# A two-layer decoder step on one core: filler products during the first loads, the first weight unit in three parts, the second unit ahead of the memory rows

## The chip, the cores and the metric

The kernel runs on one core of a Trainium2 chip. The metric is device time in microseconds (us), as the median of several runs; a measurement of this kernel can tell a difference of about 0.2% from none. A profile covers one further execution.

## What is computed

One inference step of a decoder trunk with two layers, for 256 prompt tokens and 64 sample tokens (320 columns in all) that share the weights. The part that matters here is the first layer's mixer:

```
z = x @ w_in[l] -> [q | k | v | conv h | conv B | conv C | mem q | gate_a | gate_c | gate_m]
A: sliding-window grouped-query attention with sinks
B: short gated convolution
M: 4-head cross-attention into N_MEM=256 memory tokens
   mk = mem_prompt @ w_mem_k[l];  mv = mem_prompt @ w_mem_v[l]      (256x1024 @ 1024x256, both layers)
m = sig(gate_a)*(A @ p_attn) + sig(gate_c)*(B @ p_conv) + sig(gate_m)*(M @ p_mem)
x <- LayerNorm(ALPHA * x + m @ w_o)
x <- LayerNorm(ALPHA * x + ffn(x))     dense in layer 0, 2 of 8 experts in layer 1
```

All is float32. Each product is made of three TensorE products of split operands (a high and a low part of the weights and of the activations): high x high, low weights x high, high weights x low.

## The kernel before, in words

**Units.** The weights are streamed as units of 1 MB (128 partitions x 2048 words), in the order of the list `STREAM`: two z units (each 256 columns of w_in), the four memory units (mk and mv of both layers), the other z units with p_conv, p_mem, p_attn and w_o, then the dense feed-forward, layer 1's mixer and the experts. Unit n goes into slot n mod 6 (`RING`) of `raw`. SyncE (`sp`, L653) issues the loads in that order; from the sixth on it waits until the unit that had the slot is used up (`unit_done`).

**The split of a unit.** For each unit ScalarE writes the rounded high part (`hi`, L932) and then VectorE the remainder (`lo`, L1320) in place of the raw words. Both run two units ahead of TensorE (`AHEAD`), and ScalarE's first waits until the unit three before is used up. So at the head of step i of `mixer` stand `hi(n + 2)` on ScalarE and `lo(n + 2)` on VectorE, ahead of the rest of the step.

**The start.** x arrives by three loads (two of 128 prompt rows, one of 64 sample rows). TensorE turns it in six parts of four 128-column transposes (`start_part`, L1923; k = 0, 1, 2 are the first halves of the three row blocks, 3 to 5 the second halves), ScalarE copies the high part of each (L947) and VectorE the low part (L1330). The first weight unit comes in two halves (`HALVES`), each split by ScalarE (L953) and VectorE (L1337). The memory rows (`mstage`) are loaded ahead of the second unit and turned by TensorE between the first and the second unit, in four parts more.

**The steps.** In `mixer(0)` TensorE multiplies the z units one after the other (48 products of 320 columns each). After the first it turns the memory rows; after the second (i = 1) comes `memory()`, the products of the four memory units (48 each, of 256 columns). Attention runs beside the z units: the table `SLOTS` says what follows which step. For the first of nine attention jobs (prompt rows 0 to 127 against the memory keys) it has: scores at step 1, an unrelated set of transposes of cached keys (`memk`) at step 2, and at step 3 the transposes of its probabilities (`probs`, L2004), which need the exponentials of ScalarE (L1012) and the normalisation of VectorE (L1414, L1415). VectorE does that normalisation at the next step, behind that step's `lo`.

**Banks.** Results of z units go to banks 0, 1, 2 in turn. A product into a bank waits until ScalarE has copied out the tile that was there three before (`z_cp`).

```
for i, u in enumerate(layer_units(l)):      # ScalarE
    hi(n + AHEAD)
    z_copy(l, 2 * u[2]); z_copy(l, 2 * u[2] + 1)
    ...
    if l == 0 and i == 1:
        memory()
    for work in SLOTS.get(i, ()):
```

Of the kernel before, what the change touches and what calls it, by code (L numbers as in the profile page):

```python
# [55 lines left out]
RING = 6  # L56
HI_RING = 3

HALVES = (slice(0, UNIT // 2), slice(UNIT // 2, UNIT))
RING_MOE = 11  # L60
AHEAD = HI_RING - 1

# [23 lines left out]


MEM_UNITS = [(k, l, 0) for k in ("mk", "mv") for l in range(2)]
STREAM = layer_units(0)[:2] + MEM_UNITS + layer_units(0)[2:] + ffn_units() + layer_units(1)
N_DENSE = len(STREAM)  # L90
UNIT_OF = {u: n for n, u in enumerate(STREAM)}

# [109 lines left out]
LAST_VALUES = ("pv", NJ - 1)  # L202
BETWEEN_TILES = next(i for i in SLOTS if LAST_VALUES in SLOTS[i])
assert SLOTS[BETWEEN_TILES] == [LAST_VALUES] and layer_units(0)[BETWEEN_TILES][0] == "z"
EVENTS = [x[1:] for w in sorted(SLOTS) for x in SLOTS[w] if x[0] == "event"]
N_EVENTS = len(EVENTS)
EVENT_NO = {e: n for n, e in enumerate(EVENTS)}
# [38 lines left out]
def build_trunk(nc, A, O):  # L246
    with ExitStack() as ctx:
# [20 lines left out]
        def sem(name):  # L268
            return ctx.enter_context(nc.semaphore(name))
# [178 lines left out]
        unit_done = sem("unit_done")  # L448
        zeroed = sem("zeroed")
        ld_x = [sem(f"ld_x{t}") for t in range(3)]  # L450
        ld_first = [sem(f"ld_first{h}") for h in range(2)]
        first_hi = sem("first_hi")
        first_lo = sem("first_lo")
        ld_mem = sem("ld_mem")
# [198 lines left out]

        @block.sync
        def _(sp):
            for t in range(2):
                sp.dma_start(xstage[:, t, :], A["x_prompt"][0, 128 * t:128 * t + 128, :]).then_inc(ld_x[t], 16)
            sp.dma_start(xstage[0:64, 2, :], A["x_sample"].rearrange("b t d -> (b t) d")).then_inc(ld_x[2], 16)
            for h in range(2):
                ks = slice(4 * h, 4 * h + 4)  # L660
                sp.dma_start(tiled(raw[0], 256)[:, ks], unit_source(STREAM[0])[:, ks]).then_inc(ld_first[h], 16)
            for n, u in enumerate(STREAM):
                if n == 0:
                    continue
                if n == 1:
                    for t in range(2):
                        sp.dma_start(mstage[:, t, :], A["mem_prompt"][0, 128 * t:128 * t + 128, :]).then_inc(ld_mem, 16)
                s = n % RING
# [85 lines left out]
        def _(pool):  # L754
# [34 lines left out]
                               A["cache_mem_v"][l, 4 * g:4 * g + 4].rearrange("b (k p) h d -> p (b k) (h d)", p=P)  # L789
                               ).then_inc(ld_memv, 16)  # L790

            pool.wait_ge(ld[UNIT_OF[MEM_UNITS[-1]]], 16)
            load_mem_k(0, 0)
            load_mem_v(0, 0)
            for l in range(2):
# [127 lines left out]
        def _(act):  # L923
# [22 lines left out]
                src = ps[:, bank, :].rearrange("p (f t) -> p f t", t=P)[:, :, 0:tn]  # L946
                act.activation((xh if k < X_STARTS else mTh)[:, f:f + 4, t0:t0 + tn], src, ACT.Copy).then_inc(start_hi, 1)  # L947

            for h, done in ((0, first_hi), (1, hi_done)):
                for k in range(3 * h, 3 * h + 3):  # L950
                    start_part(k)
                act.wait_ge(ld_first[h], 16)
                act.activation(high[0][:, HALVES[h]], raw[0][:, HALVES[h]], ACT.Copy).then_inc(done, 1)  # L953
            hi(1)
            act.wait_ge(const, CONSTS)

# [160 lines left out]
            def mixer(l):  # L1117
                units = layer_units(l)
                for i, u in enumerate(units):
                    n = UNIT_OF[u]  # L1120
                    hi(n + AHEAD)
                    if u[0] == "z":
                        z_copy(l, 2 * u[2])
                        if i == BETWEEN_TILES:
                            o_copy(l, NJ - 1)
                        z_copy(l, 2 * u[2] + 1)
                        if i == BETWEEN_TILES:
                            continue
                        if u[2] == 9:
                            act.wait_ge(conv_done, l + 1)  # L1130
                            act.activation(och[:, :, :], hbc[:, 4:6, :], ACT.Copy).then_inc(och_done, 1)
                    if l == 0 and i == 0:
                        for k in range(X_STARTS, len(START)):
                            start_part(k)
                        continue
                    if l == 0 and i == 1:
                        memory()
                    for work in SLOTS.get(i, ()):
                        if work[0] == "pv" and JOBS[work[1]][0] == "smem":
                            by_token(l, work[1])  # L1140
                        elif work[0] in ("pv", "turn"):
                            o_copy(l, work[1])
                        elif work[0] == "event":
                            event_copy(l, work[1:])
                        else:
                            exps(l, work[1])
                    if u[0] == "pattn":
                        for f in range(4 * u[2], 4 * u[2] + 4):
                            act.wait_ge(merge_done, l * len(MERGES) + MERGE_NO[("pattn", f)] + 1)
                            act.activation(xh[:, f, :], merged[:, f, :], ACT.Copy, scale=0.5).then_inc(mh_done, 1)  # L1150
                    if u[0] == "wo" and u[2] >= 1:
                        if u[2] == 1:
# [144 lines left out]
        def _(dve):  # L1297
# [32 lines left out]
                dve.tensor_tensor(low_part[:, f:f + 4, t0:t0 + tn], src,  # L1330
                                  high_part[:, f:f + 4, t0:t0 + tn].bitcast(F32), ALU.subtract).then_inc(start_lo, 1)

            for h, (before_it, done) in enumerate(((first_hi, first_lo), (hi_done, lo_done))):
                for k in range(3 * h, 3 * h + 3):
                    start_part(k)
                dve.wait_ge(before_it, 1)
                dve.tensor_tensor(low[0][:, HALVES[h]], raw[0][:, HALVES[h]],  # L1337
                                  high[0][:, HALVES[h]].bitcast(F32), ALU.subtract).then_inc(done, 1)
            lo(1)

            def masks():
# [218 lines left out]
            def mixer(l):  # L1560
                pending = None
                for i, u in enumerate(layer_units(l)):
# [11 lines left out]
                    if u[0] in ("pconv", "pmem"):  # L1574
                        for f in range(KD):
                            merge(l, u[0], f)
                    if l == 0 and i == 0:
                        for k in range(X_STARTS, len(START)):
                            start_part(k)
                    lo(UNIT_OF[u] + AHEAD)  # L1580
                    if l == 0 and i == 0:
                        continue
                    if l == 0 and i == 1:
                        memory()
                    if u == ("z", l, 8):
                        conv(l)
# [2 lines left out]
                    if pending is not None:  # L1589
                        normalise(l, pending)  # L1590
                        pending = None
                    for work in SLOTS.get(i, ()):
                        if work[0] == "turn" or work[0] == "pv" and JOBS[work[1]][0] != "smem":
                            o_low(l, work[1])
                        elif work[0] == "scores":
                            scores(l, work[1])
                            pending = work[1]
# [307 lines left out]
        def _(pe):  # L1905
# [20 lines left out]

            pe.wait_ge(const, 1)
            for k in range(X_STARTS):
                pe.wait_ge(ld_x[k % 3], 16)
                start_part(k)  # L1930

# [240 lines left out]
            def mixer(l):  # L2172
                for i, u in enumerate(layer_units(l)):
# [25 lines left out]
                    if side_by_side:  # L2199

                        qs = [OUT_NO[tile] for tile in tiles]
                        for k in range(KD):
                            if n == 0 and k % 4 == 0:
                                pe.wait_ge(start_lo, 3 * (k // 4) + 3)
                            if n == 0 and k == KD // 2:
                                pe.wait_ge(lo_done, 1)
                            if i > 0:
                                pe.wait_ge(ml_done, KD * l + k + 1)
# [22 lines left out]
                            first_mean(2 * l)  # L2231
                    if l == 0 or i > 1:
                        last.then_inc(unit_done, 1)
                    if l == 0 and i == 0:
                        pe.wait_ge(ld_mem, 2 * 16)
                        for k in range(X_STARTS, len(START)):
                            start_part(k)
                        continue
                    if l == 0 and i == 1:
                        memory()  # L2240
                    for work in SLOTS.get(i, ()) if i != BETWEEN_TILES else ():
                        if work[0] == "pv":
                            values(l, work[1])
                        elif work[0] == "turn":
                            turn_values(l, work[1])
                        elif work[0] == "event":
                            event(l, work[1:])
                        else:
                            scores(l, work[1])
# [272 lines left out]
```

## Time and profile before

| what | value |
|---|---|
| median of 3 runs | 1553.41 us (1552.87 to 1554.34) |
| the profiled execution | 1552.14 us |
| its span, first to last instruction | 1550.4 us |
| TensorE busy | 1520.2 us, 98% |
| VectorE, ScalarE, GpSimd busy | 1123.1, 927.2, 146.7 us |
| moved by DMA | 416.62 MB, mean 269 GB/s |

The profiled execution lies 1.27 us under the median of the runs, and 1.7 us of it lie around its span. Times in the trace are from the start of the span. "PE" is TensorE's products, "PEld" its weight loads, DVE VectorE, ACT ScalarE, SP SyncE. The listed length of a product contains its way through the array, so products that follow one another overlap: what one costs is the distance between two starts.

### The profile page before, as it was taken

Reading aid. Unit: us, or ns where it says so; the run is one execution under the profiler, and the core shown is the slowest. Engines: PE = TensorE matmul, PEld = TensorE weight load, DVE = VectorE, ACT = ScalarE, POOL = GpSimd, SP = SyncE. Lnnn points to the kernel's source line nnn. Section 1 sums busy time; section 2 is a strip of 40 time slices with the busy share of each in tenths; the row PEclk is TensorE's granted clock in tenths of the full one; section 3 lists DMA queues with packets and bytes.
Section 4 is the critical chain, followed back from the end, with each engine's and each line's share of the span. In section 5 each row is a group of like instructions: output and inputs, shape, how many; then the busy total and the mean of one; then the engine's idle time right before and its main releaser. Section 6 shows DMA issues by size and latency. Waiting matters only on the chain.

```text
span 1550.4 us, 22897 instructions
## 1 busy us (share of the span) xinstructions
PE 1520.2 (98%) x9065; PEld 1345.9 (87%) x9065; DVE 1123.1 (72%) x1044; ACT 927.2 (60%) x974; POOL 146.7 (9%) x182
## 2 busy tenths in 40 slices
PE   8999999999999999999899999999999999999996
PEld 7999999999999899999588888888888888888785
DVE  5546658844443536558698888888888888889987
ACT  5445445533333644544677777777777777777775
POOL 3203003300002103002230000000000000020000
PEclk9999999999999999999999999999999999999998
DMA  9845534695444346332799999999999999999981
GB/s 317 275 134 183 163 121 145 243 360 161 131 150 157 110 150 183 110 111 81 272 391 389 395 390 357 386 382 389 369 353 380 388 386 369 356 384 380 389 297 61
DMA packets 226425, 416.62 MB, mean 269 GB/s; under 512 B 8592, under 2 KB 110368, under 8 KB 224752
## 3 DMA queue, kind: packets, MB, share of 16 engines
q1 hardware_dynamic: 217712, 383.28, 70.2%
q0 software_dynamic: 8608, 31.89, 5.7%
q8 instruction: 73, 1.20, 0.3%
q14 instruction: 32, 0.26, 0.0%
HBM read 393.99 MB, written 23.11 MB: 269 GB/s over the span
## 4 chain that ended last, share of the span: by engine, by line
PE 95%; DVE 2%; ACT 1%; DMA 0%; issue 0%; POOL 0%; SPq 0%; DVEq 0%; POOLq 0%; ACTq 0%
PE ps L1908 13%; PE ps L1910 13%; PE ps L1909 13%; PE ps L2441 11%; PE ps L2443 11%; PE ps L2442 10%; PE ps L2425 5%; PE ps L2427 5%; PE ps L2426 5%; PE ps L2452 1%; PE ps L2004 1%; PE ps L1975 1%; PE ps L1943 0%; PE ps L1945 0%; PE ps L1944 0%; PE ps L2032 0%
## 5 line engine op out<-in xcount | busy, mean ns | idle before, releaser
L1310 DVE TENSOR_TENSOR low<-raw,high 128x2048 fp32r<-128x2048 f32 x264 | 603.8, 2291 | 88.2 <-ACT high L939 86.8
L939 ACT ACTIVATE high<-raw 128x2048 fp32r<-128x2048 f32 x264 | 505.9, 1919 | 199.8 <-PE ps L2443 126.8
L1320 DVE TENSOR_TENSOR low<-raw,high 128x2048 fp32r<-128x2048 f32 (+1 forms) x91 | 206.7, 2274 | 195.7 <-ACT high L932 195.6
L1908 PE MATMUL ps<-xh,high 128*128 128x320 f32 x1056 | 331.8, 314 | 4.3 <-DVE xl L1533 2.7
L1909 PE MATMUL ps<-xh,low 128*128 128x320 f32 x1056 | 327.0, 310 | 0.0
L1910 PE MATMUL ps<-xl,high 128*128 128x320 f32 x1056 | 326.9, 310 | 0.0
L2441 PE MATMUL ps<-high,xeh 128*128 128x512 f32 (+1 forms) x768 | 291.8, 380 | 2.7 <-ACT row_f L1239 2.5
L2443 PE MATMUL ps<-high,xel 128*128 128x512 f32 (+1 forms) x768 | 288.7, 376 | 0.0
L2442 PE MATMUL ps<-low,xeh 128*128 128x512 f32 (+1 forms) x768 | 287.5, 374 | 0.0
L932 ACT ACTIVATE high<-raw 128x2048 fp32r<-128x2048 f32 (+1 forms) x91 | 172.2, 1892 | 144.1 <-PE ps L1910 120.4
L1908 PEld LDWEIGHTS ps<-xh,high 128*128 128x128 f32 x1056 | 199.3, 189 | 10.9 <-issue 9.5
L1909 PEld LDWEIGHTS ps<-xh,low 128*128 128x128 f32 x1056 | 199.5, 189 | 0.2
L1910 PEld LDWEIGHTS ps<-xl,high 128*128 128x128 f32 x1056 | 199.1, 189 | 0.0
L2441 PEld LDWEIGHTS ps<-high,xeh 128*128 128x128 f32 x768 | 144.4, 188 | 31.3 <-issue 2.7
L2443 PEld LDWEIGHTS ps<-high,xel 128*128 128x128 f32 x768 | 144.2, 188 | 28.9
L2442 PEld LDWEIGHTS ps<-low,xeh 128*128 128x128 f32 x768 | 144.1, 188 | 27.4
L2425 PE MATMUL ps<-high,heh 128*128 128x512 f32 x352 | 141.2, 401 | 0.0
L2427 PE MATMUL ps<-high,hel 128*128 128x512 f32 x352 | 138.4, 393 | 0.0
L2426 PE MATMUL ps<-low,heh 128*128 128x512 f32 x352 | 138.4, 393 | 0.0
L2427 PEld LDWEIGHTS ps<-high,hel 128*128 128x128 f32 x352 | 66.3, 188 | 15.3
L2425 PEld LDWEIGHTS ps<-high,heh 128*128 128x128 f32 x352 | 66.2, 188 | 14.2 <-issue 0.2
L2426 PEld LDWEIGHTS ps<-low,heh 128*128 128x128 f32 x352 | 66.3, 188 | 13.7
(388 smaller groups left out, 1664.8 us busy)
## 6 DMA issues: line engine op xcount, KB each, us to landing
raw<-in_exp_w_gate_dram SPq DMA_DIRECT2D x88, 1024.0 KB, 7.7
raw<-in_exp_w_up_dram SPq DMA_DIRECT2D x88, 1024.0 KB, 7.7
raw<-in_exp_w_down_dram SPq DMA_DIRECT2D x88, 1024.0 KB, 7.1
raw<-in_w_in_dram SPq DMA_DIRECT2D x37, 1024.0 KB, 5.3
ybuf<-zeros POOLq DMA_DIRECT2D x12, 1024.0 KB, 19.7
raw<-in_ffn_w_gate_dram SPq DMA_DIRECT2D x11, 1024.0 KB, 5.4
raw<-in_ffn_w_up_dram SPq DMA_DIRECT2D x11, 1024.0 KB, 6.5
raw<-in_w_o_dram SPq DMA_DIRECT2D x8, 1024.0 KB, 5.1
```

The costliest lines, as they stand in the source:

```text
L939: act.activation(high[(N_DENSE + m) % HI_RING][:, :], raw_moe[s][:, :], ACT.Copy).then_inc(hi_done, 1)
L1310: dve.tensor_tensor(low_moe[s][:, :], raw_moe[s][:, :], high[(N_DENSE + m) % HI_RING][:, :].bitcast(F32), ALU.subtract).then_inc(lo_done, 1)
L1320: dve.tensor_tensor(low[n % RING][:, cols], raw[n % RING][:, cols], high[n % HI_RING][:, cols].bitcast(F32), ALU.subtract).then_inc(lo_don ...
L1908: pe.matmul(out, wh, ah, start=first, stop=False)
L1909: pe.matmul(out, wl, ah, start=False, stop=False)
L1910: return pe.matmul(out, wh, al, start=False, stop=last)
L2425: pe.matmul(out, heh[:, tile, :], wh[:, c], start=i == 0 and k == 0, stop=False)
L2426: pe.matmul(out, heh[:, tile, :], wl[:, c], start=False, stop=False)
L2427: last = pe.matmul(out, hel[:, tile, :], wh[:, c], start=False, stop=i == NBLK - 1 and k == 1)
L2441: pe.matmul(out, xeh[:, k, slots], wh[:, c], start=k == 0, stop=False)
L2442: pe.matmul(out, xeh[:, k, slots], wl[:, c], start=False, stop=False)
L2443: last = pe.matmul(out, xel[:, k, slots], wh[:, c], start=False, stop=k == KD - 1)
```

## The change

- TensorE multiplies the identity by itself (128x128) ahead of the first three start parts, 6, 2 and 4 times, with a result that nothing reads (`WARM_UP`).
- The first unit is loaded and split in three parts (k = 0 and 1, 2 and 3, 4 to 7). The first of them is loaded ahead of the sample rows, and ScalarE and VectorE split a part between the start parts. TensorE begins the unit when the first part is split.
- SyncE loads the second unit ahead of the memory rows, and the third z unit ahead of the four memory units.
- TensorE turns the memory rows behind the second unit instead of the first, and `memory()` follows the third unit (i = 2). What `SLOTS` had for step 1 and step 2 of layer 0 now both follows step 2.

```
-HALVES = (slice(0, UNIT // 2), slice(UNIT // 2, UNIT))
+FIRST_PARTS = ((0, 2), (2, 4), (4, KD))
+FIRST_COLUMNS = tuple(slice(256 * k0, 256 * k1) for k0, k1 in FIRST_PARTS)
+WARM_UP = (6, 2, 4)
...
-STREAM = layer_units(0)[:2] + MEM_UNITS + layer_units(0)[2:] + ffn_units() + layer_units(1)
+STREAM = layer_units(0)[:3] + MEM_UNITS + layer_units(0)[3:] + ffn_units() + layer_units(1)
...
+def beside(l, i):
+
+    if l == 0 and i < 3:
+        return SLOTS[1] + SLOTS[2] if i == 2 else []
+    return SLOTS.get(i, [])
...
             for t in range(2):
                 sp.dma_start(xstage[:, t, :], A["x_prompt"][0, 128 * t:128 * t + 128, :]).then_inc(ld_x[t], 16)
+            first_part(0)
             sp.dma_start(xstage[0:64, 2, :], A["x_sample"].rearrange("b t d -> (b t) d")).then_inc(ld_x[2], 16)
-            for h in range(2):
-                ks = slice(4 * h, 4 * h + 4)
-                sp.dma_start(tiled(raw[0], 256)[:, ks], unit_source(STREAM[0])[:, ks]).then_inc(ld_first[h], 16)
+            first_part(1)
+            first_part(2)
...
-                if n == 1:
+                if n == 2:
                     for t in range(2):
                         sp.dma_start(mstage[:, t, :], A["mem_prompt"][0, 128 * t:128 * t + 128, :]).then_inc(ld_mem, 16)
...
+            start_part(0)
+            start_part(1)
+            first_part(0, first_hi)
+            start_part(2)
+            first_part(1, first_hi)
+            for k in range(3, 6):
+                start_part(k)
+            first_part(2, hi_done)
...
-                    if l == 0 and i == 0:
+                    if l == 0 and i == 1:
                         for k in range(X_STARTS, len(START)):
                             start_part(k)
-                        continue
-                    if l == 0 and i == 1:
+                    if l == 0 and i == 2:
                         memory()
-                    for work in SLOTS.get(i, ()):
+                    for work in beside(l, i):
...
             for k in range(X_STARTS):
+                for _ in range(WARM_UP[k] if k < 3 else 0):
+                    pe.matmul(ps[:, 1, 0:P], ident[:, :], ident[:, :], start=True, stop=True)
                 pe.wait_ge(ld_x[k % 3], 16)
                 start_part(k)
```

Three places in the order of the instructions. The first is the start of the program on TensorE, before and after; `xstage` holds the rows of x, `ident` the identity.

```order
L1904 UNCONDITIONAL_BRANCH
L1923 MATMUL ps<-ident,xstage 128x128 x8
L1923 MATMUL ps<-ident,xstage 128x64 x4
L1923 MATMUL ps<-ident,xstage 128x128 x8
L1923 MATMUL ps<-ident,xstage 128x64 x4
```

```order
L1932 UNCONDITIONAL_BRANCH
L1958 MATMUL ps<-ident 128x128 x6
L1951 MATMUL ps<-ident,xstage 128x128 x4
L1958 MATMUL ps<-ident 128x128 x2
L1951 MATMUL ps<-ident,xstage 128x128 x4
L1958 MATMUL ps<-ident 128x128 x4
L1951 MATMUL ps<-ident,xstage 128x64 x4
L1951 MATMUL ps<-ident,xstage 128x128 x8
L1951 MATMUL ps<-ident,xstage 128x64 x4
```

Twelve identity products have come in between; all 24 transposes still stand ahead of the first product of the first unit.

The second place is TensorE behind the last product of the memory units: before, then now. L2025 (now L2055) are the scores of the first attention job, L1975 (L2005) the transposes of cached keys, L2004 (L2034) those of the job's probabilities; each left-out stretch is one z unit.

```order
L2025 MATMUL ps<-mkT,qmT 128x256 x4
L1908 MATMUL ps<-xh,high_61 128x320
...
L1975 MATMUL ps<-ident,kstage 128x128 x8
L1908 MATMUL ps<-xh,high_62 128x320
...
L2004 MATMUL ps<-ident,sc 128x128 x8
```

```order
L2055 MATMUL ps<-mkT,qmT 128x256 x4
L2005 MATMUL ps<-ident,kstage 128x128 x8
L1936 MATMUL ps<-xh,high_62 128x320
...
L2034 MATMUL ps<-ident,sc 128x128 x8
```

Between the scores and the transposes of the probabilities stand one z unit now, and two before.

The third place is ScalarE at the same point, from the copy of the second layer's memory keys on: before, then now. `sc<-ps` are the exponentials of the first job, `mem_kT` the copy of the turned cached keys, `high` the high part of a unit.

```order
L963 ACTIVATE mkT<-ps 128x512
L932 ACTIVATE high_62<-raw_50 128x2048
L1012 ACTIVATE sc,small<-ps,small 128x256 x4
L932 ACTIVATE high_63<-raw_51 128x2048
L1038 ACTIVATE qT<-ps 64x256
...
L970 ACTIVATE mem_kT<-ps 128x1024
```

```order
L985 ACTIVATE mkT<-ps 128x512
L947 ACTIVATE high_63<-raw_51 128x2048
L1034 ACTIVATE sc,small<-ps,small 128x256 x4
L992 ACTIVATE mem_kT<-ps 128x1024
L947 ACTIVATE high_61<-raw_52 128x2048
L1063 ACTIVATE kvT<-ps 128x320 x2
```

The copy of the cached keys now stands between the exponentials and the next high part. On VectorE the rows are the same as before there: low part of that unit, then reciprocal and normalisation.

## Rows read from the trace of the kernel before

**Rows 1.** The page: busy times; the chain that ended last, by engine.
```profile
PE 1520.2 (98%) x9065; PEld 1345.9 (87%) x9065; DVE 1123.1 (72%) x1044; ACT 927.2 (60%) x974; POOL 146.7 (9%) x182
...
PE 95%; DVE 2%; ACT 1%; DMA 0%; issue 0%; POOL 0%; SPq 0%; DVEq 0%; POOLq 0%; ACTq 0%
```

**Rows 2.** Waits of PE, whole span: total, times, longest, in us.
```profile
PE ps L1908 <- DVE xl L1533: 2.7, 1, 2.7
```

**Rows 3.** Timeline of PE, 0 to 23 us: start, length, instructions [idle before them].
```profile
4.57 1.09 PE L1923 MATMUL ps<-ident,xstage 128*128 128x128 f32 x4 [4.57 <-DMA xstage<-in_x_prompt_dram]
...
8.55 3.20 PE L1923 MATMUL ps<-ident,xstage 64*128 64x64 f32 x16 [1.36 <-DMA xstage<-in_x_sample_dram]
12.22 0.61 PE L1908 MATMUL ps<-xh,high 128*128 128x320 f32 x1 [0.48 <-issue]
...
15.56 0.45 PE L1908 MATMUL ps<-xh,high 128*128 128x320 f32 x1
15.83 0.34 PE L1909 MATMUL ps<-xh,low 128*128 128x320 f32 x1
...
20.99 1.91 PE L1923 MATMUL ps<-ident,mstage 128*128 128x128 f32 x16
22.65 0.39 PE L1908 MATMUL ps<-xh,high 128*128 128x320 f32 x1
```

**Rows 4.** Windows: busy us of PE, PEld, DVE, ACT, POOL; PEclk, DMA share, GB/s.
```profile
6.00:8.00 2.00, 1.12 (x4) 0.72 (x4) 0.84 (x2) 0.89 (x2) 0.72 (x2) 1.00 0.97 218
8.00:10.00 2.00, 1.45 (x8) 1.33 (x9) 0.86 (x2) 0.57 (x2) 0.00 (x0) 1.00 1.11 354
```

**Rows 5.** Timelines of ACT and DVE, 9 to 23 us.
```profile
9.81 1.06 ACT L953 ACTIVATE high<-raw 128x1024 fp32r<-128x1024 f32 x1 [0.15 <-DMA raw<-in_w_in_dram]
...
20.17 1.92 ACT L932 ACTIVATE high<-raw 128x2048 fp32r<-128x2048 f32 x1 [1.15 <-DMA raw<-in_w_mem_k_dram]
...
22.25 0.43 ACT L1050 ACTIVATE qm_diag<-ps 64x64 f32<-64x64 f32 x2
...
9.69 0.42 DVE L1330 TENSOR_TENSOR xl<-ps,xh 128x256 fp32r<-128x256 f32 x1 [1.14 <-ACT xh L947]
10.90 1.23 DVE L1337 TENSOR_TENSOR low<-raw,high 128x1024 fp32r<-128x1024 f32 x1 [0.79 <-ACT high L953]
```

**Rows 6.** Timeline of PE, 53 to 70 us: from the first scores to their probabilities.
```profile
53.65 1.14 PE L2025 MATMUL ps<-mkT,qmT 64*128 64x256 f32 x8
54.71 0.41 PE L1908 MATMUL ps<-xh,high 128*128 128x320 f32 x1
...
61.86 1.04 PE L1975 MATMUL ps<-ident,kstage 128*128 128x128 f32 x8
62.65 0.39 PE L1908 MATMUL ps<-xh,high 128*128 128x320 f32 x1
...
69.77 0.49 PE L2004 MATMUL ps<-ident,sc 128*128 128x128 f32 x3
```

**Rows 7.** Timeline of DVE, 54 to 67 us.
```profile
54.36 0.23 DVE L1367 COPY vecs<-ps 128x76 f32<-128x76 f32 x1
...
57.35 1.22 DVE L1381 TENSOR_REDUCE small<-ps 128x4 f32<-128x1024 f32 x1
...
62.58 2.29 DVE L1320 TENSOR_TENSOR low<-raw,high 128x2048 fp32r<-128x2048 f32 x1 [3.80 <-ACT high L932]
...
64.99 1.22 DVE L1415 TENSOR_TENSOR sc<-sc,small 128x1024 f32<-128x1024 f32 x1
```

**Rows 8.** Timeline of ACT, 60 to 66 us.
```profile
60.63 1.92 ACT L932 ACTIVATE high<-raw 128x2048 fp32r<-128x2048 f32 x1
...
64.59 1.03 ACT L970 ACTIVATE mem_kT<-ps 128x1024 f32<-128x1024 f32 x1
```

**Rows 9.** The end: PE's last product (timeline); one window with its PEclk.
```profile
1536.02 0.39 PE L2395 MATMUL ps<-ygl,slot 128*128 128x512 f32 x1
...
1541.00:1542.00 1.00, 0.00 (x0) 0.00 (x0) 1.00 (x1) 1.00 (x3) 0.00 (x0) 0.81 0.00 0
```

More of the change, by code:

```diff
@@ L450, in build_trunk @@
         ld_x = [sem(f"ld_x{t}") for t in range(3)]
-        ld_first = [sem(f"ld_first{h}") for h in range(2)]
+        ld_first = [sem(f"ld_first{h}") for h in range(3)]
         first_hi = sem("first_hi")
@@ L655, in _, with first_part @@
         def _(sp):
+            def first_part(h):
+                ks = slice(*FIRST_PARTS[h])
+                sp.dma_start(tiled(raw[0], 256)[:, ks], unit_source(STREAM[0])[:, ks]).then_inc(ld_first[h], 16)
             for t in range(2):
                 sp.dma_start(xstage[:, t, :], A["x_prompt"][0, 128 * t:128 * t + 128, :]).then_inc(ld_x[t], 16)
+            first_part(0)
             sp.dma_start(xstage[0:64, 2, :], A["x_sample"].rearrange("b t d -> (b t) d")).then_inc(ld_x[2], 16)
-            for h in range(2):
-                ks = slice(4 * h, 4 * h + 4)
-                sp.dma_start(tiled(raw[0], 256)[:, ks], unit_source(STREAM[0])[:, ks]).then_inc(ld_first[h], 16)
+            first_part(1)
+            first_part(2)
             for n, u in enumerate(STREAM):
@@ L790, in load_mem_v @@
                                ).then_inc(ld_memv, 16)
-            pool.wait_ge(ld[UNIT_OF[MEM_UNITS[-1]]], 16)
+            pool.wait_ge(ld[UNIT_OF[MEM_UNITS[-1]] % RING], LD_VALUE[UNIT_OF[MEM_UNITS[-1]]])
             load_mem_k(0, 0)
@@ L947, in start_part, with first_part @@
                 act.activation((xh if k < X_STARTS else mTh)[:, f:f + 4, t0:t0 + tn], src, ACT.Copy).then_inc(start_hi, 1)
-            for h, done in ((0, first_hi), (1, hi_done)):
-                for k in range(3 * h, 3 * h + 3):
-                    start_part(k)
+            def first_part(h, done):
                 act.wait_ge(ld_first[h], 16)
-                act.activation(high[0][:, HALVES[h]], raw[0][:, HALVES[h]], ACT.Copy).then_inc(done, 1)
+                act.activation(high[0][:, FIRST_COLUMNS[h]], raw[0][:, FIRST_COLUMNS[h]], ACT.Copy).then_inc(done, 1)
+            start_part(0)
[6 more added lines that the diff above has]
+            first_part(2, hi_done)
             hi(1)
@@ L1331, in start_part, with first_part @@
                                   high_part[:, f:f + 4, t0:t0 + tn].bitcast(F32), ALU.subtract).then_inc(start_lo, 1)
[L1333 to L1338, printed above, removed]
+            def first_part(h, done):
+                c = FIRST_COLUMNS[h]
+                dve.tensor_tensor(low[0][:, c], raw[0][:, c], high[0][:, c].bitcast(F32), ALU.subtract).then_inc(done, 1)
+            start_part(0)
+            start_part(1)
+            dve.wait_ge(first_hi, 1)
+            first_part(0, first_lo)
+            start_part(2)
+            dve.wait_ge(first_hi, 2)
+            first_part(1, first_lo)
+            for k in range(3, 6):
+                start_part(k)
+            dve.wait_ge(hi_done, 1)
+            first_part(2, lo_done)
             lo(1)
@@ L1576, in mixer @@
                             merge(l, u[0], f)
-                    if l == 0 and i == 0:
+                    if l == 0 and i == 1:
                         for k in range(X_STARTS, len(START)):
@@ L1580, in mixer @@
                     lo(UNIT_OF[u] + AHEAD)
-                    if l == 0 and i == 0:
-                        continue
-                    if l == 0 and i == 1:
+                    if l == 0 and i == 2:
                         memory()
@@ L1591, in mixer @@
                         pending = None
-                    for work in SLOTS.get(i, ()):
+                    for work in beside(l, i):
                         if work[0] == "turn" or work[0] == "pv" and JOBS[work[1]][0] != "smem":
@@ L2204, in mixer @@
                                 pe.wait_ge(start_lo, 3 * (k // 4) + 3)
-                            if n == 0 and k == KD // 2:
+                            if n == 0 and k == FIRST_PARTS[1][0]:
+                                pe.wait_ge(first_lo, 2)
+                            if n == 0 and k == FIRST_PARTS[2][0]:
                                 pe.wait_ge(lo_done, 1)
@@ L2233, in mixer @@
                         last.then_inc(unit_done, 1)
-                    if l == 0 and i == 0:
+                    if l == 0 and i == 1:
                         pe.wait_ge(ld_mem, 2 * 16)
@@ L2237, in mixer @@
                             start_part(k)
-                        continue
-                    if l == 0 and i == 1:
+                    if l == 0 and i == 2:
                         memory()
-                    for work in SLOTS.get(i, ()) if i != BETWEEN_TILES else ():
+                    for work in beside(l, i) if i != BETWEEN_TILES else ():
                         if work[0] == "pv":
```

## The prediction

> **What bounds the kernel now.** I read the page first. TensorE is busy for 98% of the span, and 95% of the chain that ended last is its work [rows 1]. So time can go only where TensorE idles or runs slowly, and whatever makes it wait anew is added to the end one for one. The list of TensorE's waits came next. Its longest wait outside the start is 2.7 us, at a layer norm [rows 2]; that one is measured from TensorE's own last product, so it moves with TensorE and absorbs nothing. No transfer comes at a fixed time later on either: SyncE's loads wait for units that TensorE has used up.
>
> The timeline of TensorE shows what the start costs. Nothing runs until 4.57 us, when the first rows of x are there. The sample rows land at 8.55 us; from then 16 transposes take 3.20 us, and the first product of the first unit starts at 12.22 us [rows 3]. At that moment the low part of the unit's first half has just ended on VectorE (10.90 + 1.23 = 12.13) [rows 5]. The first products start 0.27 us apart: 13 lie between 12.22 and 15.83 us (0.267 us each for 320 columns, which is the level of 1.2 GHz), and the remaining 35 take 5.16 us, 0.147 us each, the level of 2.4 GHz [rows 3]. The column of the granted clock reads 1.00 at 6 to 10 us already [rows 4], so here the spacing is the evidence and not that column. Transposes did not raise the rate: 24 of them ran between 4.57 and 11.75 us.
>
> The last place is where the change joins two steps of attention. Scores of the first job start at 53.65, TensorE reaches the transposes of its probabilities at 69.77 [rows 6], and VectorE has had them ready since 64.99 + 1.22 = 66.21 us [rows 7]. That slack of 3.6 us is what I set against the unit that the change takes out from between.
>
> **The start, part by part.** The 12 identity products cost no more than the idle time in which they stand. A 128-column transpose takes about (1.09 - 0.42) / 3 = 0.22 us at the low rate [rows 3]; the identity products have the same shape, so I take 0.22 us and double it as an upper bound. Six are 1.3 us (bound 2.6) inside the 4.57 us before x. Two are 0.45 us and four 0.9 us (bounds 0.9 and 1.8) ahead of the next two landings; the gap before the sample rows is 1.36 us [rows 3] and they now land later, so nothing is pushed by more than 0.4 us even at the bounds.
>
> Loads: 256 KB of the first unit now pass ahead of the sample rows. At 354 GB/s that is 0.74 us, at 218 GB/s 1.2 us [rows 4], and nothing if the transfers in flight share the engines anyway. I take 0.4 us: sample rows at 8.95 us. All 16 transposes behind them still stand ahead of the first unit. At the low rate they end at 8.95 + 3.20 = 12.15 us. The first part of the unit is then long split (it needs half of 1.06 + 1.23 us behind its landing [rows 5]), so the three parts take VectorE's work off this path, but the path through the transposes is as long. First product at 12.15 instead of 12.22: a gain of **0.1 us**, between -0.7 and +0.4.
>
> The rest of the head: the second unit lands before the memory rows instead of behind them, which is earlier than it is needed. The 16 transposes of the memory rows (1.66 us, from 20.99 to 22.65 [rows 3]) move behind the second unit, the third unit (7.1 us) moves ahead of the memory units: neither is added or removed. SyncE issues one load more, hidden, since its queue is ahead of the engines. GpSimd's load of cached keys waits for the last memory unit, which is now the seventh unit; the keys are first needed after all memory units, some 20 us behind that landing. Cost nothing; without that cover it would be what the load is late by.
>
> **The joined steps.** From the start of the scores, TensorE needs 54.71 - 53.65 = 1.06 us for them, 62.65 - 61.86 = 0.79 for the cached keys and 69.77 - 62.65 = 7.12 for one z unit [rows 6]: it reaches the probabilities 8.97 us behind the start of the scores. The cached keys' transposes also need VectorE's copy that ends at 54.36 + 0.23 = 54.59 us [rows 7]; TensorE gets there at 54.71, so this costs about nothing.
>
> The other engines' chain starts at the same moment. VectorE first ends the sum of x and reduces the scores from 57.35 us [rows 7]; exponentials; then ScalarE makes the next unit's high part from 60.63 us for 1.92 us, VectorE its low part (62.58, 2.29 us) and only then the normalisation, ready at 66.21, 12.56 us behind the scores [rows 7, 8]. Nothing in that chain is shortened, and one thing is put in: ScalarE's copy of the cached keys (1.03 us listed, about 0.95 in a row of others [rows 8]) now stands between the exponentials and that high part. So the probabilities are ready 12.56 + 0.95 + 0.1 (signalling) = 13.6 us behind the scores. TensorE waits 13.6 - 8.97 = **4.6 us**; bounds 4.4 and 4.8. Queued behind it are the next scores and unit four, all on the chain. Later jobs keep their two units of distance, so the wait comes once and isn't won back.
>
> **Sum.** Against the profiled execution: 1552.14 + 4.6 - 0.1 = 1556.6 us. The median of the runs lies 1.27 us above that execution, which I carry over: 1553.41 + 4.5 = **1557.9 us**.
>
> **Where a rule speaks otherwise.** The trace shows a rate that stayed low through transposes and rose 3.6 us after the first true product [rows 3]. The Trainium skill, page "TensorE: Matmul & The Clock Gate" (Part 4), says that transposes don't count as activity for the clock gate; by that rule, the trace agrees, and the identity products, which are no transposes, could count. The same page (Part 1) says that the moment of the rise differs from run to run, which the one execution here can't show. By the rule the start could run at the high rate; that is the first rival, worked out from rows.
>
> **Rivals.**
> *A, the rate is high when the sample rows land.* Then 16 transposes take 1.66 us [rows 3], first product near 8.95 + 1.7 = 10.7 us (the sample rows' low part, 1.56 us behind the landing by 10.11 - 8.55, allows it [rows 3, 5]). First unit 48 x 0.147 = 7.1 us, to 17.8. But the second unit's second tile needs a bank that ScalarE frees only behind the third unit's high part: if that unit lands where the third one did, at 20.17, the copy ends at 22.25 + 0.43 = 22.7 us [rows 5]; half a unit behind it is 26.2. Before, two units would end at 20.99 + 7.1 = 28.1. Gain 1.9 us, at most 3.2 if the landing is earlier: 1553.41 + 4.6 - 1.9 = 1556.1, down to 1554.8. For: products were issued. Against: they fill 0.22 x 12 = 2.6 of the first 9 us, in three bursts with idle time between. Chance 0.29.
> *B, the clock falls during the new wait.* At the end of the span TensorE's last product ends at 1536.4, and the window 1541 to 1542 reads 0.81, so the fall from 2.4 to 1.2 GHz came near 1541.6, 5.2 us later [rows 9]; a wait of 2.7 us [rows 2] did nothing of the kind. 4.6 us lie between. If it falls, the next 13 products or twice as many cost 0.12 us more each: 1.6 to 3.1 us, 1559.5 to 1561.0. Chance 0.12.
> *C, faster: the wait is covered.* The place is the transposes of the first job's probabilities. It would need the normalisation to be ready 9.0 us behind the scores rather than 13.6, by VectorE or ScalarE being some 4.6 us less late than their queues show. Then only the start's gain is left, with the high rate 1.9 us or more: 1551.5, down to 1550.2. For it speaks only that the slack before was 3.6 us; against, that a whole unit of 7.1 us leaves the stretch. Chance 0.07.
> *D, the change does little of what it says:* some of the wait is covered and the start is unchanged, 1553.5 to 1556. Chance 0.06.
>
> **The numbers.** Forecast 0.46. Slower by over 0.2% is above 1556.5 us: nearly all of the forecast (0.43), B (0.12) and a third of A (0.10) make 0.65. Within 0.2%: the rest of A (0.19), of the forecast (0.03) and D, 0.28. Faster: C, 0.07. The range goes from 1554.3, which leaves out C and a little of A and D, to 1560.3, which leaves out the upper half of B.
>
> **What would show it.** Right: an idle time of TensorE of 4.4 to 4.8 us at the transposes of the first probabilities (L2034), released by VectorE's normalisation; the first 320-column product near 12.15 us, with a spacing of 0.27 us for about 3.6 us. A would show as a spacing of 0.147 us from the first product on. B would show as 0.27 us spacing in the unit behind the wait. The prediction is wrong if TensorE passes L2034 without idling, if the start gives more than 2 us, or if a new wait stands at the second unit or at the memory units.

## The result, and the profile after

| | before | changed |
|---|---|---|
| median, 7 runs each | 1553.41 us | 1559.14 us |
| lowest and highest | 1552.10 to 1555.54 | 1558.03 to 1559.57 |
| span of the profiled execution | 1550.4 us | 1557.4 us |

The ratio to the kernel before is 1.0037, 95% interval 1.0027 to 1.0046: slower by 5.7 us. The forecast was 1557.9 us (1554.3 to 1560.3).

The list of TensorE's waits in the changed kernel (line waiting, what released it; total, times, longest in us):

```profile
PE ps L2034 <- DVE sc L1445: 4.4, 1, 4.4
PE ps L1936 <- DVE xl L1563: 3.4, 1, 3.4
...
PE ps L1936 <- ACT qm_diag L1072: 0.9, 1, 0.9
...
PE ps L1936 <- DVE low L1341: 0.2, 1, 0.2
```

The first row was not there before: the transposes of the first job's probabilities wait for VectorE's normalisation. The third and fourth stand at the second unit. The second is the layer norm wait of [rows 2] (2.7 us there); it comes out at 2.7 or at 3.4 us in the profiles of all kernels here, with and without the change, so I don't count it as a part of the change.

TensorE's timeline at the start, changed kernel:

```profile
1.61 2.93 PE L1958 MATMUL ps<-ident 128*128 128x128 f32 x12 [1.61 <-POOL ident L778]
...
6.85 1.06 PE L1958 MATMUL ps<-ident 128*128 128x128 f32 x8
9.01 1.88 PE L1951 MATMUL ps<-ident,xstage 64*128 64x64 f32 x16 [1.11 <-DMA xstage<-in_x_sample_dram]
10.82 0.41 PE L1936 MATMUL ps<-xh,high 128*128 128x320 f32 x1
11.07 0.31 PE L1937 MATMUL ps<-xh,low 128*128 128x320 f32 x1
...
18.34 0.41 PE L1936 MATMUL ps<-xh,high 128*128 128x320 f32 x1 [0.22 <-DVE low L1341]
...
23.06 0.41 PE L1936 MATMUL ps<-xh,high 128*128 128x320 f32 x1 [0.93 <-ACT qm_diag L1072]
...
26.69 1.91 PE L1951 MATMUL ps<-ident,mstage 128*128 128x128 f32 x16
```

Against [rows 3]: the 16 transposes behind the sample rows take 1.88 instead of 3.20 us, the first product of the first unit starts at 10.82 instead of 12.22, and the products behind it follow at the high rate. The unit is done 3 us earlier. Two new waits in the second unit, 1.15 us of idle time, take 1.6 us of that back from start to start: the transposes of the memory rows start at 26.69 us, and before, the same two units without those transposes would have been done at 28.1. The row of six identity products counts twelve: a float32 product of this kind leaves two records, a transpose one.

TensorE's timeline where the steps are joined, changed kernel:

```profile
59.23 1.14 PE L2055 MATMUL ps<-mkT,qmT 64*128 64x256 f32 x8
60.29 1.09 PE L2005 MATMUL ps<-ident,kstage 128*128 128x128 f32 x8
...
68.12 0.31 PE L1938 MATMUL ps<-xl,high 128*128 128x320 f32 x1
72.86 1.94 PE L2034 MATMUL ps<-ident,sc 128*128 128x128 f32 x8 [4.44 <-DVE sc L1445]
74.73 2.08 PE L2055 MATMUL ps<-mkT,qmT 64*128 64x256 f32 x8
76.74 1.84 PE L2005 MATMUL ps<-ident,kstage 128*128 128x128 f32 x8
78.34 0.39 PE L1936 MATMUL ps<-xh,high 128*128 128x320 f32 x1
```

Its chain on the other engines, ScalarE first, then VectorE:

```profile
66.21 1.03 ACT L992 ACTIVATE mem_kT<-ps 128x1024 f32<-128x1024 f32 x1
67.12 1.93 ACT L947 ACTIVATE high<-raw 128x2048 fp32r<-128x2048 f32 x1
...
69.08 2.29 DVE L1341 TENSOR_TENSOR low<-raw,high 128x2048 fp32r<-128x2048 f32 x1 [4.71 <-ACT high L947]
...
71.49 1.22 DVE L1445 TENSOR_TENSOR sc<-sc,small 128x1024 f32<-128x1024 f32 x1
```

The copy of cached keys, the high part, the low part and the normalisation follow each other without a gap, and TensorE waits for the last of them. The windows of one microsecond over the same place (busy us of PE, PEld, DVE, ACT, POOL; granted clock, DMA share, GB/s):

```profile
70.00:71.00 1.00, 0.00 (x0) 0.00 (x0) 1.00 (x1) 0.00 (x0) 0.00 (x0) 1.00 0.36 81
71.00:72.00 1.00, 0.00 (x0) 0.00 (x0) 0.97 (x3) 0.00 (x0) 0.00 (x0) 0.74 1.63 603
72.00:73.00 1.00, 0.14 (x1) 0.17 (x2) 0.72 (x1) 0.00 (x0) 0.00 (x0) 0.50 0.72 257
```

While TensorE idled, its clock fell from 2.4 to 1.2 GHz (1.00 to 0.50), before the work came back. A mean of 0.74 between 71 and 72 us puts the fall near 71.5, 3.1 us behind the end of TensorE's last product (68.12 + 0.31). So transposes, scores and keys behind the wait take 5.48 us (72.86 to 78.34), and the next unit runs at the high rate again. Before, they began at 69.77 [rows 6] and the next unit's first product stood at 72.77:

```profile
72.77 0.39 PE L1908 MATMUL ps<-xh,high 128*128 128x320 f32 x1
```

That is the profile of before, 3.00 us. The account of the two profiled executions up to this unit, the fifth z unit: scores reached 1.57 us earlier than they would have been (59.23 against 53.65 + 7.15 for the unit moved ahead of them); wait 4.66 (the 4.44 us shown and the end of the last product); slow stretch 2.48; together 5.57, which is 78.34 - 72.77.

The two executions differ by 7.0 us at their ends, so 1.5 us arise later. They come from the layer norm wait and from falls of the clock away from the changed places. The kernel before has such a fall at its own largest wait outside the start, the one at the layer norm. One row of its timeline and one of its windows:

```profile
511.33 0.60 PE L1908 MATMUL ps<-xh,high 128*128 128x320 f32 x1 [2.70 <-DVE xl L1533]
511.00:512.00 1.00, 0.67 (x2) 0.70 (x3) 0.96 (x3) 0.38 (x1) 1.00 (x2) 0.50 0.00 0
```

The clock reads 0.50 there, and the products behind the wait stand 0.267 us apart until 514.1 us. In the changed kernel this wait is 0.7 us longer (first product behind it at 517.56 us, 6.23 later than before). Further falls stand near 746 us in the kernel before, and near 775 us in the changed kernel, where the kernel before has none. The first costs the kernel before 0.9 us, the second costs the changed kernel 1.5.

### The profile page after: what moved, and what is told of

Read it like the earlier page. It is cut to its first block, busy times and chain, and to the rows that moved or that the text cites. A ratio compares the mean times of both kernels' runs of the same rounds, so it can differ in the third digit from the quotient of the medians.

```text
span 1557.4 us, 22947 instructions
## 1 busy us (share of the span) xinstructions
PE 1524.7 (98%) x9089; PEld 1350.0 (87%) x9089; DVE 1124.2 (72%) x1045; ACT 927.5 (60%) x975; POOL 145.0 (9%) x182
## 4 chain that ended last, share of the span: by engine, by line
PE 93%; DVE 3%; ACT 1%; DMA 1%; issue 1%; SPq 0%; POOL 0%; DVEq 0%; ACTq 0%; POOLq 0%
PE ps L1936 13%; PE ps L1937 12%; PE ps L1938 12%; PE ps L2472 11%; PE ps L2474 11%; PE ps L2473 10%; PE ps L2456 5%; PE ps L2458 5%; PE ps L2457 5%; PE ps L2483 1%; DMA raw<-in_w_in_dram 1%; PE ps L2034 1%; PE ps L2005 1%; PE ps L1973 0%; PE ps L1975 0%
```

## The experiments

Every kernel was run on the same chip beside the kernel before; "ratio" is to that kernel, with its 95% interval.

**e1, normalisation ahead of the low part.** The edit, on VectorE in the changed kernel:

```
+                    if l == 0 and i == 3:
+                        normalise(l, pending)
+                        pending = None
                     lo(UNIT_OF[u] + AHEAD)
```

> The changed kernel with one thing moved: at step 3 of layer 0 VectorE normalises the first job's probabilities ahead of the low part of unit 9 instead of behind it. Theory (the wait before the probabilities is the chain high part, low part, normalisation, and the clock falls only because of that wait): the normalisation is then ready about 66.3 + 1.4 = 67.8 us, before TensorE arrives at 68.4; no wait at the probabilities' transposes, no fall of the clock, and the time is 4.4 + 2.2 = 6.7 us below the changed kernel, about 1552.4, which is 1.0 to 1.4 us below the kernel before. Rival 1 (the wait only moves, since the low part now comes 1.4 us later or something else is late next): a wait of over 1 us at a neighbouring place, time above 1554. Rival 2 (the joined steps are innocent and the loss lies elsewhere): time stays within 1 us of 1559.1.

Measured: 1553.25 us against 1553.34, ratio 0.9997 (0.9988 to 1.0006). VectorE's timeline:

```profile
67.02 1.23 DVE L1445 TENSOR_TENSOR sc<-sc,small 128x1024 f32<-128x1024 f32 x1
69.53 2.29 DVE L1341 TENSOR_TENSOR low<-raw,high 128x2048 fp32r<-128x2048 f32 x1 [1.28 <-ACT high L947]
```

The probabilities are ready at 68.25 us, TensorE takes them up at 68.71 without waiting, and the low part starts when its high part is there, as before. 5.9 us are gone, all of the loss. What the medians don't show is the 1.0 to 1.4 us below the kernel before. A part of it is not gained: the two waits at the second unit are longer than in the changed kernel:

```profile
PE ps L1939 <- ACT qm_diag L1072: 1.3, 1, 1.3
...
PE ps L1939 <- DVE low L1341: 0.5, 1, 0.5
```

The rest is there in the profiled execution, where the fifth z unit starts at 71.96 us, 0.81 earlier than before, and so does all work up to the layer norm. It is lost behind that, most of it at 767 us, where the clock fell in this execution (0.77 from 766 to 767 us, 0.50 behind it) and not in that of the kernel before. Whether it is lost so in most executions, one profile can't tell.

**e2, TensorE kept at work during the wait.** Ahead of the waiting transposes:

```
+                    if l == 0 and i == 3:
+                        pe.wait_ge(z_cp, 6)
+                        for _ in range(20):
+                            pe.matmul(ps[:, 2, 0:P], ident[:, :], ident[:, :], start=True, stop=True)
```

> The changed kernel with 20 identity products on TensorE ahead of the waiting transposes of the first probabilities (about 0.11 us each, 2.2 of the 4.4 us of the wait). The wait itself stays in length. Theory (the idle time made the clock fall, and this cost 2.2 us of the loss by itself): the 320-column products behind stay 0.147 us apart, granted clock 1.00 throughout, time about 2.2 us below the changed kernel, 1556.9. Rival (the lower rate behind the wait has another cause, or a shorter idle time still makes it fall): transposes and scores behind the wait take 5.5 us as in the changed kernel, time 1559.1.

Measured: 1557.73 us, ratio 1.0027 (1.0017 to 1.0037), 1.4 us below the changed kernel. The fillers were dearer than I had them, 0.23 us each, and filled the whole wait:

```profile
68.94 4.63 PE L2275 MATMUL ps<-ident 128*128 128x128 f32 x40
73.54 1.06 PE L2034 MATMUL ps<-ident,sc 128*128 128x128 f32 x8
```

VectorE's normalisation ended at 72.17 + 1.22 = 73.39 us in it, so they made it no longer. The clock stayed at 1.00, and the transposes take 1.06 instead of 1.94 us. So the fall of the clock is a consequence of the idle time. It cost 1.4 us in the medians, whose intervals overlap (1.0017 to 1.0037 against 1.0027 to 1.0046). In the profiles, from the scores to the fifth z unit, it cost 2.45 (16.66 us here, 19.11 in the changed kernel). What a shorter idle time does, this run doesn't tell, since none was left.

**e3, the changed kernel without identity products** (`WARM_UP = (0, 0, 0)`).

> The changed kernel without its 12 identity products at the start. Theory (they alone raise the rate before the sample rows land): the 16 transposes take 3.2 us again, the first 320-column product starts near 12.2 us instead of 10.8, products 0.267 us apart for 3 to 4 us; but the wait for the bank in the second unit (0.9 us) and for its low part (0.2 us) then vanish, so of 3.0 us in the first unit only 1.4 are lost: time 1560.5. Rival (the loads in another order and the three parts make the gain): time within 0.4 us of the changed kernel.

Measured: 1558.84 us, ratio 1.0036 (1.0024 to 1.0048), level with the changed kernel, which is the rival's number. The start did as my theory had it, though:

```profile
8.71 3.20 PE L1951 MATMUL ps<-ident,xstage 64*128 64x64 f32 x16 [1.83 <-DMA xstage<-in_x_sample_dram]
11.85 0.63 PE L1936 MATMUL ps<-xh,high 128*128 128x320 f32 x1
12.28 0.47 PE L1937 MATMUL ps<-xh,low 128*128 128x320 f32 x1
```

The memory rows were turned at 27.91 us instead of 26.69, and the scores began 1.2 us later. But the clock fell later in this execution's wait (at 74.0) and was back sooner: the stretch from the probabilities to the fifth z unit took 4.51 us instead of 5.48. So the fall blurs what the start is worth, and e3 can't settle it.

**e4, the new start alone.** The changed kernel with `STREAM`, memory rows, `memory()` and `beside` put back as before.

> The kernel before with the new start alone: identity products and the first unit in three parts, its first part ahead of the sample rows; memory rows, memory units and the attention steps stand as before. Theory (start's gain is whole where nothing is joined, no wait at the probabilities): first product near 10.8 us at the high rate, first unit done 3.0 us earlier; but the memory rows and the second unit land no earlier than before (second unit at 17.1 us, its low part by 21.4), so TensorE may wait for it from 17.9 + 1.7 = 19.6 us to 21.4: a gain of 1.2 to 1.3 us, time 1552.2. Rival (the second unit lands earlier or is not waited for): gain 3.0 us, 1550.4. Rival (the start is worth nothing): 1553.4.

Measured: 1553.42 us, ratio 1.0001 (0.9992 to 1.0010): none of the 1.2 us that I had expected, and the number of the last rival. The start itself came as forecast, with the first product at 10.97 us at the high rate. The waits of TensorE in its profile show where it went:

```profile
PE ps L1974 <- DVE low L1340: 1.7, 1, 1.7
...
PE ps L1937 <- DVE low L1340: 1.2, 1, 1.2
```

One, foreseen, at the second unit; a second, not foreseen, at the first memory unit. Its low part stands behind the memory rows' start parts on VectorE, and those behind the high part that waits for this unit's landing.

**e5, early normalisation and early copy.** e1, and on ScalarE at the head of the step:

```
+                    if n == 0:
+                        z_copy(l, 0)
+                        z_copy(l, 1)
                     hi(n + AHEAD)
+                    if n == 0:
+                        continue
```

> The kernel with the early normalisation and one more thing moved: at step 0 of layer 0 ScalarE copies the first unit's two tiles out ahead of the third unit's high part, which waits for its landing at about 20.5 us. Theory (with the new start TensorE gets ahead only to stand at the bank of the second unit's second tile, 1.3 us, which is why the early normalisation alone ended level with the kernel before): that wait goes, the one for the second unit's low part (0.5 us) stays, and the time falls by 1.3 us against the early normalisation alone, to about 1552.0, ratio to the kernel before 0.9991. Rival (the gained time is waited for again at the third unit or the memory units, which land no earlier): 1553.3, with a new wait for a low part in the first 40 us.

Measured: 1551.17 us against 1553.62, ratio 0.9986 (0.9977 to 0.9995): the only kernel here whose interval lies below 1. The difference is 0.16%, under the 0.2% named above; the profile has it too, with the fifth z unit at 70.32 us, 2.45 earlier than before. Behind the start of the second unit nothing waits until the memory rows:

```profile
18.36 0.41 PE L1944 MATMUL ps<-xh,high 128*128 128x320 f32 x1 [0.34 <-DVE low L1346]
...
25.51 1.91 PE L1959 MATMUL ps<-ident,mstage 128*128 128x128 f32 x16
```

**e6, e1 without identity products.**

> The kernel with the early normalisation, without the 12 identity products at the start. Here no fall of the clock at the attention step blurs what they are worth. Theory (they move the rise of the rate ahead of the sample rows, and the wait for the bank takes most of it back): first 320-column product near 11.9 us with 0.267 us between products for about 4 us, no wait for the bank, memory rows turned about 1.2 us later: 1554.4. Rival (worth nothing, since the runs without and with them were 1558.8 and 1559.1): 1553.3. Rival (worth their full 3.0 us): 1556.3.

Measured: 1553.31 us, ratio 0.9995 (0.9986 to 1.0005), against 1553.25 for e1. In the medians, what the identity products are worth with the bank wait in place can't be told from nothing. The profiles show the 1.1 us of my first line: the memory rows are turned at 28.18 us here and at 27.01 in e1, and the fifth z unit starts at 73.13 and 71.96, 1.17 us apart. Behind the layer norm the two executions had their falls of the clock at different places.

**e7, the join alone.** The kernel before with only `beside` of the change.

> The kernel before with the join alone: start, loads and the memory units' place as before, but the first scores follow the third unit's products and stand directly ahead of the cached keys' transposes. Theory (the wait is a chain against one unit of cover): VectorE has then finished the sum of x long before, so the chain from the scores is about 2.6 us shorter (13.6 - 2.6 = 11.0 against 9.0 of cover): a wait of about 2.0 us at the transposes of the probabilities, no fall of the clock, 1555.4. So of the 4.4 us, 2.6 would come from having the memory units directly ahead of the scores. Rival (the join costs the whole 4.4 us wherever it stands): 1557.8 or more. Rival (the join by itself is covered): 1553.4.

Measured: 1555.56 us against 1553.62, ratio 1.0013 (1.0004 to 1.0022), 1.9 us. The wait in its profile, and VectorE's reduction of the scores, which no longer stands behind the sum of x:

```profile
PE ps L2013 <- DVE sc L1424: 1.9, 1, 1.9
...
61.42 1.22 DVE L1390 TENSOR_REDUCE small<-ps 128x4 f32<-128x1024 f32 x1 [2.22 <-PE ps L2034]
```

So the join costs 1.9 us by itself; with the memory units directly ahead of the scores, VectorE comes to them 2.5 us later (62.94 - 59.23 against 61.42 - 60.23), and the wait is 4.4 us.

**e8, e5 without identity products.**

> The kernel with early normalisation and early copy, without the 12 identity products. Theory (they are worth 1.3 us of transposes and 1.6 us of slow products, and it shows only where no bank wait takes it back): first 320-column product near 12.0 us, rate up near 16, memory rows turned near 28.0 us instead of 25.5, time 1551.2 + 2.5 = 1553.7, level with the kernel before. Rival (the early copy is what gained, the identity products are worth nothing): 1551.2.

Measured: 1553.64 us, ratio 1.0003 (0.9994 to 1.0012), 2.5 us above e5, as expected. So in the medians they are worth 2.5 us without the bank wait, and nothing that can be told with it (e6). The profile of e8 doesn't show the course that I had put down for it: the memory rows were turned at 26.47 us and not near 28.0, only 0.96 later than in e5. In this execution the rate rose 1.1 us behind the first product (12.98 against 11.88), in the other four without identity products 2.8 to 4.3 us behind it, so the moment differs from run to run.

**e9, the kernel before with identity products alone.**

> The kernel before with the 12 identity products as its only change. Theory (the loads and splits behind the start stand where they were): the rate is high from the first product, but that product still waits for the low part of the unit's first half at 12.1 us, and the second unit's low part is still ready at 21.3 us only, so of 1.6 us gained in the first unit about 1.3 us are left at most: 1552.1 to 1553.4. Rival (nothing behind the start limits): 1551.8 or less, with no wait for a low part in the first 40 us.

Measured: 1552.53 us, ratio 0.9996 (0.9987 to 1.0005): not to be told from no change. Its profile shows more than was asked. The products start at the high rate, then the clock falls under them:

```profile
6.29 1.06 PE L1930 MATMUL ps<-ident 128*128 128x128 f32 x8
8.16 1.87 PE L1923 MATMUL ps<-ident,xstage 64*128 64x64 f32 x16 [0.81 <-DMA xstage<-in_x_sample_dram]
11.80 0.39 PE L1908 MATMUL ps<-xh,high 128*128 128x320 f32 x1 [1.77 <-issue]
...
12.00:13.00 1.00, 1.00 (x6) 1.00 (x6) 1.00 (x3) 0.64 (x1) 0.00 (x0) 0.57 0.99 368
```

Its first product still waits for the low part of half a unit, which ends at 11.69 us; in the changed kernel (10.82) and in e4 (10.97) it does not. So the three parts close the gap behind the transposes, and there the clock stayed up.

**All kernels side by side.** Start of the fifth z unit in the profiled execution, against 72.77 us in the kernel before, and the median, against that of the kernel before on the same chip:

| | fifth z unit, us | difference | difference of the medians |
|---|---|---|---|
| changed | 78.34 | +5.57 | +5.7 |
| e1 | 71.96 | -0.81 | -0.1 |
| e2 | 76.56 | +3.79 | +4.4 |
| e3 | 78.58 | +5.81 | +5.5 |
| e4 | 73.10 | +0.33 | +0.1 |
| e5 | 70.32 | -2.45 | -2.45 |
| e6 | 73.13 | +0.36 | -0.3 |
| e7 | 74.37 | +1.60 | +1.9 |
| e8 | 71.30 | -1.47 | +0.3 |
| e9 | 72.23 | -0.54 | -0.8 |

From this unit to the layer norm the distances stay within 0.1 us. Behind it each profile adds its own, by the length of that wait and by falls of the clock between 508 and 522, 746 and 757, and 766 and 778 us. Every profile has the first; some have the second, some the third. From the fifth z unit to the end the difference to the kernel before changes by 0.05 us in e4 and by 2.4 in e5 and e8, and that is as much as most of the differences at the start. So e5's profile ends level with that of the kernel before, and only the medians show it faster at the end.

## Why the prediction was right, and where it was not

**The wait: right, in place and size.** Forecast 4.6 us at L2034 behind the normalisation; shown 4.44, 4.66 from start to start. The chain was put at 13.6 us from the scores; it is 72.86 - 59.23 = 13.63. e1 changes nothing but the order of two pieces of work on VectorE and removes the loss. That the wait comes once, as the forecast had it, holds: no other wait over 0.3 us stands behind it up to 90 us.

**The start: wrong.** The step was "First product at 12.15 instead of 12.22: a gain of 0.1 us". It came at 10.82, at the high rate: that was rival A, with 0.29. The 0.1 us stood on the rate staying low until the first true product, as before; the runs show it high from the first product on wherever the identity products and the three parts stand together. I had held against it that the identity products fill only 2.6 us in three bursts. Each was also mis-sized: not 0.22 but 0.45 us at the low rate (six in 2.93 us), by the two records each leaves, so my doubled bound was the value. Rival A's own sum was near: gain 1.9 us by a bank wait at the second unit's second tile, shown 1.57 with that very wait (0.93 us). One sign that I had named for the prediction being wrong came true here: a new wait stands at the second unit. In the medians this gain doesn't show: e1 ends level with the kernel before.

**The clock: wrong in the likeliest case.** Rival B (0.12), the fall during the wait, happened. It cost 2.48 us in the profile, inside the 1.6 to 3.1 us that I gave, and 1.4 us in the medians by e2, just under it. The cost fell on the transposes and scores behind the wait, and not on the 320-column products of the unit, as I had it. I had given B little by a wrong reading: "a wait of 2.7 us [rows 2] did nothing of the kind". The trace of the kernel before shows the opposite at this very wait, 0.50 at 511 us and products 0.267 us apart behind it. With that row read, the fall would have been the likely case for a wait of 4.6 us. (A smaller slip: 13 products in 3.61 us are 0.278 us each; 0.267 holds from the second on, the first distance being 0.41.)

**The sum** came near by luck in part. I had 4.6 - 0.1 + 0 = 4.5 us; the profiles show 4.66 for the wait, -1.57 at the start and +2.48 for the clock, 5.57 in all. The two errors have opposite signs. The forecast named slower for the right main cause, with the wrong course at the start and at the clock.

The Trainium skill, page "TensorE: Matmul & The Clock Gate" (Part 4), says that transposes don't count as activity for the clock. e9 fits this and doesn't prove it: the clock fell near 12.1 us, 4.8 us behind the last identity product, though 16 transposes ran in between; but 1.8 us of idle time stood there as well. I had cited the rule and given it too little weight against three short bursts.

## What to carry to other kernels

When work is taken out from between a producer and its consumer, count the cover that is left on the waiting engine against the other engines' whole queue, and not only against the operations that the consumer needs: here 9.0 us of cover stood against 13.6 us, of which 4.2 us were the split of a unit not needed yet, and to let the normalisation go first cost nothing. An earlier start is worth something only as far as the next due times have room: 3 us gained in the first unit left 0.8 us at the fifth z unit (e1), and 2.45 when a copy that stood behind a late load was moved ahead of it (e5). An idle time of TensorE costs more than its length if the clock falls in it, so read the granted clock around every long wait before you say what a wait does to it. And where single executions differ by up to 2.4 us through such falls, compare the profiles up to the first of them beside the medians.

## What the runs showed of the hardware

- The granted clock fell 3.1 us behind the end of TensorE's last product in the changed kernel (68.4 to 71.5), 4.4 us in e3 and 5.2 us at the end of the kernel before [rows 9]. At the layer norm wait of the kernel before it fell only 2.2 us behind it (508.6 to 510.8), behind some short products of 80 columns; it fell at this wait, or up to 1.1 us behind its end, in the profiles of all kernels here. It didn't fall in e2, where fillers took the wait of 4.6 us, nor in e7, where the wait was 1.9.
- A float32 product of the identity by itself (128 columns, no transpose) leaves two records, each the length of a transpose: 0.45 us a product at 1.2 GHz, 0.23 us at 2.4 GHz (20 in 4.63 us). Twelve of them at the start raised the rate before x was complete in all six profiles that had them, and 24 transposes alone in none of the five without.
- The column of the granted clock read 1.00 at 12 to 13 us in all five profiles without identity products, while 320-column products stood 0.267 us apart in them; later falls (at 71.5, and at 12.1 us in e9) it shows. At the start the distance of products is what can be trusted.
